# A decoder layer on eight cores: other order and other issue times for the input projections, gate chunks from attention step 8 instead of 14

## The reference, cut to what matters

```python
h = rms_norm(x, norm_mix)                       # x: [2048, 1024] per core
q, k, v, u, g_a, g_p = split(h @ w_in)          # q, k, v, u: 512 columns each; gates: 1024 each
q = rope(rms_norm_per_head(q)); k = rope(rms_norm_per_head(k))
o_attn = moba_attention(q, k, v)                # own block of 256 plus up to 3 selected past blocks
o_pool = multiscale_pool(u)                     # windows 2, 4, 8, 16 minus the token, per-group linear
m = sigmoid(g_a) * (o_attn @ w_up_attn) + sigmoid(g_p) * (o_pool @ w_up_pool)
x = x + m @ w_out
x = x + relu(rms_norm(x) @ w_ff1)**2 @ w_ff2
```

## Time and profile before

| | |
|---|---|
| time, median of 3 runs | 940.35 us (939.48 to 942.74) |
| the profiled execution's own time | 939.31 us |
| span shown by its profile (slowest core) | 938.0 us |
| spans of the 8 cores | 932.2 to 938.0 us |
| granted TensorE clock, mean per core | 0.993 to 1.000 |
| PE busy | 901.4 us (96%) |
| DVE busy | 457.4 us (49%) |
| ACT busy | 368.8 us (39%) |

### The profile page before, as it was taken

One profiled execution on the slowest core, in us unless ns is written; L12 is line 12 of the kernel. 1 busy time (PEld: TensorE's weight loads), 2 busy tenths in 40 slices (PEclk: granted clock), 3 DMA queues, 4 the chain that ended last, 5 costly groups with the idle time before them and its releaser, 6 DMA issues.

```text
span 938.0 us, 17381 instructions; the slowest of 8 cores (932.2 to 938.0 us)
## 1 busy us (share of the span) xinstructions
PE 901.4 (96%) x5724; PEld 461.7 (49%) x5724; DVE 457.4 (49%) x858; ACT 368.8 (39%) x730; POOL 113.2 (12%) x201
## 2 busy tenths in 40 slices
PE   2899998899999999999999999999999999999998
PEld 1444454567777764444444444444444444444444
DVE  2788875656423234334774444444444443444444
ACT  2677545798999962221006234031111221111220
POOL 4212211221000000100101111001110111000000
PEclk9999999999999999999999999999999999999999
DMA  8963342234443444993997434014330333201113
GB/s 199 216 147 88 62 130 52 53 42 83 81 72 58 70 79 107 192 201 80 171 135 117 51 51 55 14 24 56 47 55 1 44 47 57 35 1 68 68 68 157
DMA packets 66341, 78.12 MB, mean 83 GB/s; under 512 B 35984, under 2 KB 54672, under 8 KB 66000
## 3 DMA queue, kind: packets, MB, share of 16 engines
q0 software_dynamic: 25056, 40.28, 29.3%
q1 hardware_dynamic: 41200, 36.75, 16.3%
HBM read 98.41 MB, written 8.39 MB: 114 GB/s over the span
## 4 chain that ended last, share of the span: by engine, by line
PE 89%; DMA 4%; DVE 2%; issue 2%; ACT 2%; DVEq 0%; POOL 0%; ACTq 0%; POOLq 0%; SPq 0%
PE bank L1372 24%; PE bank L1343 24%; PE bank L1013 11%; PE bank L433 9%; PE bank L907 6%; PE bank L1243 6%; PE bank L945 3%; PE bank L1027 3%; PE bank L1032 3%; DMA raw<-x 2%; DMA raw<-w_slice 1%; DMA raw<-w_qkvu 1%; PE bank L487 1%; PE bank L520 1%; DVE raw L461 0%
## 5 line engine op out<-in xcount | busy, mean ns | idle before, releaser
L1350 ACT ACTIVATE raw<-bank 128x512 f32<-128x512 f32 x128 | 76.4, 597 | 375.6 <-PE bank L1343 316.9
L1372 PE MATMUL bank<-raw 128*128 128x512 bf16 (+1 forms) x1032 | 223.2, 377 | 0.0
L1343 PE MATMUL bank<-raw 128*128 128x512 bf16 x1024 | 223.1, 379 | 0.0
L1372 PEld LDWEIGHTS bank<-raw 128*128 128x128 bf16 x1032 | 101.0, 98 | 120.2
L1343 PEld LDWEIGHTS bank<-raw 128*128 128x128 bf16 x1024 | 100.2, 98 | 120.8
L1352 DVE SCALAR_TENSOR_TENSOR raw<-bank,raw 128x512 bf16<-128x512 f32 x128 | 88.6, 692 | 140.6 <-ACT raw L1350 140.6
L914 ACT ACTIVATE raw<-bank 128x512 bf16<-128x512 f32 (+1 forms) x288 | 146.1, 591 | 21.7 <-PE bank L945 20.6
L1380 DVE SCALAR_TENSOR_TENSOR raw<-bank,raw 128x512 f32<-128x512 f32 x129 | 96.3, 747 | 112.5 <-PE bank L1372 112.0
L433 PE MATMUL bank<-raw 128*128 128x512 bf16 x512 | 122.8, 390 | 9.6 <-ACT raw L372 4.0
L1013 PE MATMUL bank<-raw 128*128 128x512 bf16 x512 | 122.5, 379 | 0.7 <-DMA raw<-w_slice 0.7
L907 PE MATMUL bank<-raw 128*128 128x256 bf16 x576 | 98.4, 266 | 2.4 <-ACT raw L914 1.9
(11 more groups left out here) (91 smaller groups left out, 578.5 us busy)
## 6 DMA issues: line engine op xcount, KB each, us to landing
raw<-x SPq DMA_DIRECT2D x32, 512.0 KB, 6.9
raw<-w_ff POOLq DMA_DIRECT2D x64, 256.0 KB, 4.0
raw<-w_slice POOLq DMA_DIRECT2D x22, 640.0 KB, 7.8
out<-raw SPq DMA_DIRECT2D x15, 512.0 KB, 2.6
raw<-w_qkvu POOLq DMA_DIRECT2D x8, 512.0 KB, 12.9
raw<-raw SPq DMA_DIRECT2D x2, 1024.0 KB, 4.8
raw<-w_out POOLq DMA_DIRECT2D x4, 512.0 KB, 13.7
raw<-c_ind POOLq DMA_DIRECT2D x4, 256.0 KB, 4.3
```

The source lines that it names most:

```text
L1343: t.group("pe", [lambda e, c=c, j=j, bk=bk: e.matmul(bank_f(bk), lhsT=ffw1[s][:, c, j * 128:(j + 1) * 128], rhs=hT[:, c, tg * 512:(tg + 1) ...
L1350: t.op("act", lambda e, bk=bk, si_=si_: e.activation(out=sqz[si_], in_=bank_f(bk), func=AF.Square), reads=hb[bk], writes=[b_sqz[si_]])
L1372: t.group("pe", [lambda e, j=j, bk=bk, i=i, c0_=c0_, c1_=c1_, n_=n_: e.matmul(bank_f(bk)[:, 0:n_], lhsT=a1T[ab][:, j, i * 128:(i + 1) * 12 ...
```

## The change

In the first loads, x tile 1 is issued on SP at once, ahead of the wait for K's weights, and V's weights on POOL directly behind the memsets, without a wait for x. The lag of V falls from 3 rounds to 2, that of Q rises from 7 to 8. The U jobs, until now 12 rounds behind K with the last five after all Q jobs, stand in rounds 5, 6, 7, 8, 10 and so on up to 23, every one ahead of the last Q job. U's weights are asked for ahead of Q's, and the band's constants earlier. The planner's assumed arrival times and first free times are other numbers. Gate chunks start at step 8 instead of 14; 92 chunks are still spread up to the same last step, so their distance grows from 3.02 to 3.08 steps.

```diff
-        U_LAG = 12
+        Q_LAG = 8
+        u_round = [int(5.0 + 1.25 * tt) for tt in range(NT)]
         jobs = []
-        for r in range(NT + 7):
-            for cg, lag in ((CG_K, 0), (CG_V, 3), (CG_U, U_LAG), (CG_Q, 7)):
+        for r in range(NT + Q_LAG):
+            for cg, lag in ((CG_K, 0), (CG_V, 2)):
                 if 0 <= r - lag < NT:
                     jobs.append((cg, r - lag))
-        u_rest = list(range(NT + 7 - U_LAG, NT))
+            jobs += [(CG_U, tt) for tt in range(NT) if u_round[tt] == r]
+            if 0 <= r - Q_LAG < NT:
+                jobs.append((CG_Q, r - Q_LAG))
         NJ_Q = len(jobs)
...
             load_w(CG_K)
+            p0_load(1)
             pool_setup()
+            load_w(CG_V)
             t.wait_written("sp", b_wqkvu[CG_K][0])
-            p0_load(1)
             p0_load(2)
...
             p0_load(3)
-            t.wait_written("pool", b_xslot[1])
-            load_w(CG_V)
...
-        W_AT = {CG_K: 15.0, CG_V: 30.0, CG_Q: 43.0, CG_U: 54.0}
-        X_AT = [4.7, 16.3, 18.6, 23.0]
+        W_AT = {CG_K: 14.8, CG_V: 26.0, CG_U: 38.0, CG_Q: 48.0}
+        X_AT = [4.9, 11.5, 17.5, 21.5]
...
-        add("wq", 4.0, [("pool", 2.0, lambda: load_w_after(CG_Q, 0))], deps=[muls[1]], after=26.0)
-        add("wu", 8.0, [("pool", 2.0, lambda: load_w_after(CG_U, 1))], deps=[muls[2]], after=34.0)
+        add("wu", 4.0, [("pool", 2.0, lambda: load_w_after(CG_U, 0))], deps=[muls[1]], after=25.0)
+        add("wq", 8.0, [("pool", 2.0, lambda: load_w_after(CG_Q, 2))], deps=[muls[3]], after=34.0)
...
-        G_START = 14
+        G_START = 8
```

More of the change, by code:

```diff
@@ L417, in p0_ev @@
                   hb[bk], [b_hT[tt]])
-        U_LAG = 12
+        Q_LAG = 8
+        u_round = [int(5.0 + 1.25 * tt) for tt in range(NT)]
         jobs = []
-        for r in range(NT + 7):
-            for cg, lag in ((CG_K, 0), (CG_V, 3), (CG_U, U_LAG), (CG_Q, 7)):
+        for r in range(NT + Q_LAG):
+            for cg, lag in ((CG_K, 0), (CG_V, 2)):
                 if 0 <= r - lag < NT:
                     jobs.append((cg, r - lag))
-        u_rest = list(range(NT + 7 - U_LAG, NT))
+            jobs += [(CG_U, tt) for tt in range(NT) if u_round[tt] == r]
+            if 0 <= r - Q_LAG < NT:
+                jobs.append((CG_Q, r - Q_LAG))
         NJ_Q = len(jobs)
-        for tt in u_rest:
-            jobs.append((CG_U, tt))
+        jobs += [(CG_U, tt) for tt in range(NT) if u_round[tt] >= NT + Q_LAG]
         NJ = len(jobs)
@@ L748, in build_nc @@
         by_job = dict(zip(jobs, pj_of))
-        add("wq", 4.0, [("pool", 2.0, lambda: load_w_after(CG_Q, 0))], deps=[muls[1]], after=26.0)
-        add("wu", 8.0, [("pool", 2.0, lambda: load_w_after(CG_U, 1))], deps=[muls[2]], after=34.0)
-        add("band_ld", 12.0, [("pool", 1.0, lambda: t.dma("pool", band, c_band_d, writes=[b_band]))], after=40.0)
+        add("wu", 4.0, [("pool", 2.0, lambda: load_w_after(CG_U, 0))], deps=[muls[1]], after=25.0)
+        add("wq", 8.0, [("pool", 2.0, lambda: load_w_after(CG_Q, 2))], deps=[muls[3]], after=34.0)
+        add("band_ld", 6.0, [("pool", 1.0, lambda: t.dma("pool", band, c_band_d, writes=[b_band]))], after=27.0)
         add("wg_ld", 20.0, [("pool", 1.0, lambda: t.dma("pool", wgT_f, w_grpT_d, writes=[b_wgTf]))], after=60.0)
@@ L769, in build_nc @@
         free_at = {n_: {i: 0.0 for i in v_} for n_, v_ in pools.items()}
-        eng_free = {"pe": 0.0, "act": 0.0, "dve": 0.0, "pool": 20.0, "sp": 22.0}
+        eng_free = {"pe": 0.0, "act": 0.0, "dve": 0.0, "pool": 17.0, "sp": 21.0}
         INF = 1e18
@@ L1131, in build_nc @@
                 done.add("u")
-                assert si <= 17, si
+                assert si <= 7, si
                 u_done()
```

## The result

The changed kernel is slower: 955.8 us where the prediction has 936.5. Its runs took 950.51, 955.77 and 958.47 us, against a median of 940.61 before; the ratio is 1.0159 (95%: 1.0130 to 1.0188). Two more of its runs, with one die at a lower clock, are left out of every comparison. The profiled execution took 955.77; its slowest core is core 0, its cores spread from 945.8 to 954.7 (before 932.2 to 938.0).

The account below looks back on a forecast made before the run. PE work was taken to bound the kernel, so only its idle time could be won. Four terms, -4.6 + 7.8 - 5.5 - 1.5, gave -3.8: 935.5 us for this execution, 936.5 by the median; 8-in-10 range 930 to 943.

Parts of the forecast that it names:

- What bounds the kernel: Whole kernel: PE work is 89% of the chain, so reordering can win only time in which PE stands still.
- Term 1: Start, up to the 14th finished job: x tile 9 lands at 46, the job ends at 53, -4.6 us (-6.6 to +1.4).
- The third case: Start: V's weights make x tiles land later, tile 9 at 53, sum +5.9, about 946 us; chance 0.20.
- there is room: Start, against the later-tiles case: bytes up to tile 9 are unchanged and the DMA share of the first 60 us is 0.91.
- The cover for K of tile 0: Start: K of tile 0, now held back by tile 1, costs nothing unless tile 1 lands after 13.
- The rule beside it: DMA at the start: engines take turns between queues packet by packet, so V's early issue takes turns from x tiles 2 and 3.
- Term 2: Middle, 14th job to end of last Q job: five more U jobs there, 99.5 against 91.7 us, +7.8 (6.8 to 10.5).
- Term 3: Attention's beginning, last Q job to 18th exponential: ACT's four waits for PE go, -5.5 us (-6.6 to -1).
- My sign of being wrong: Attention's beginning: a granted clock under 0.9 for more than 10 us behind the last Q job would show the forecast wrong.
- The second case: Attention's beginning: without filler PE runs at half speed to the 18th step, sum +0.7, about 941 us; chance 0.26.
- Term 4: Gate chunks: 1.7 more chunks done by step 46 are missing later, where PE is full, -1.5 us (0 to -1.7).

Follow-up runs that it names:

- h2: g1 with V's weights issued without a wait, the order on every engine held fixed: 944.5 us, ratio 1.0057.
- g1: Kernel before with x tile 1 ahead of the wait for K's weights, V's weights behind the landing of x tile 2: 941.7 us, ratio 1.0015.
- h3: f2 with V's weights waiting for x tile 2 again, the planner's order held fixed: 946.3 us, ratio 1.0076.
- f2: Kernel before with only the changed first loads (x tile 1 and V without waits) and their arrival numbers: 948.0 us, ratio 1.0083.
- f4: Changed kernel with the first loads and arrival numbers of before and chunks from step 14, so the order of jobs and weights alone: 946.3 us, ratio 1.0062.
- k5: Kernel before with its own first loads but g1's arrival numbers, so g1's order on every engine: 945.3 us, ratio 1.0061.
- h4: f4 with 25 more products that nobody reads, placed where PE stood still at attention's beginning: 946.1 us, ratio 1.0073.
- h1: f4 with the U jobs spread from round 9 instead of 5, four of them behind the last Q job: 939.9 us, ratio 1.0008.
- k1: Changed kernel with two buffers for the attention outputs instead of one, no load or product moved: 949.8 us, ratio 1.0094.
- g4: f4 with gate slice 1 loaded at step 13 instead of 5: 951.6 us, ratio 1.0115.
- k4: Kernel before with two buffers for the attention outputs instead of one: 939.8 us, ratio 0.9995.

## Why the prediction was wrong

**What bounds the kernel.** That held, as far as PE sets the time: in the ledger the lost PE time goes from 33.2 to 49.6 us up to 260, and the mean span of the cores from 935.5 to 950.0.

**Term 1, the start: -4.6 predicted, +6.6 measured** (64.2 against 57.6). This is the first step that failed. x tile 1 landed at 12.3 (11.5 predicted), and SP's next issue came 1.4 later, as said (1.5). What failed is "up to there x tiles 2 and 3 get the other share ... tiles 7, 8 and 9 take 4.6 each". I took the equal bytes of the earlier trace rows, where both queues had long been busy, for the rate at any time. Where a weight load has just started, x tiles issued 1 to 2.3 us behind it get 0.00 to 0.02 MB in 3 us (15 to 18, 36 to 39; h2 against g1 in one order). Up to tile 6 little is lost by it, 34.5 against my 32. Tile 7 then lands at 46.7, 12.1 behind tile 6 where I had 4.6, and tiles 8 and 9 follow 3.8 and 4.9 behind: 7.5 of the 9.4 us arise at tile 7. The constants behind tile 2 are late too: the rope table lands at 28.8, before at 21.3. The trace of the kernel before had shown it; DMA queues of its core 3, 24 to 25.5, just behind the start of V's weights, with an x tile under way since 23.84:

```profile
q0 software_dynamic: 63, 0.24, 96.4%
q1 hardware_dynamic: 3, 0.00, 0.9%
```

Of the 11.2 us between -4.6 and +6.6, tile 9's landing makes 9.4; the other 1.8 are the step from tile 9 to the 14th job, 8.8 instead of 7. The third case named this mechanism and its point of decision, a landing at 52.5; it came at 55.4, and its formula for the whole sum, landing minus 49.8, would have given +5.6, about 945 for this execution. I gave it 0.20, because "there is room" by the mean DMA share; a mean over 60 us says nothing about the 3 us in which a queue stands.

Nor is the transfer the whole. The order that the planner makes of the new numbers cost 2.4 us with V free, as in the change, and 5.7 with V waiting (h2, h3, g1, f2), and the new order of jobs 3.8 in the first 60 us with before's loads (f4: 24.5 against 20.7); the prediction had no term for either. "The cover for K of tile 0 ... costs nothing unless tile 1 lands after 13" was right, and k5 shows the other side: tile 1 at 16.5 there, and a 9.35 us wait.

**The rule beside it.** The Trainium skill, "DMA: Bandwidth & Descriptors", section "Queues, rings and completion order", has each engine take turns between the queues that have work. The stretches above speak against turns of equal size just behind the start of a weight load: 0.50 against 0.02 MB. Whether the x tiles' queue had work on those engines at that time, no trace here shows. I said that the rule spoke against the change, and its direction was right.

**Term 2: +7.8 predicted, +8.5 measured** (164.3 less 64.2 is 100.1, against 91.7). A little high, inside its range of 6.8 to 10.5, and right.

**Term 3: -5.5 predicted, -6.3 measured** (18.8 against 25.05). The size was right, in part by luck: I had all four waits of ACT gone, and two of 1.59 and 0.81 us are there; but the first exponential comes 4.5 us behind the last Q job where before it came 6.5. My sign of being wrong, a granted clock under 0.9 for more than 10 us, came without the loss: 0.74 from 164 to 184. f4 bears terms 2 and 3 out: over the cores with all matmuls on record they come to +1.9 there (+7.2 and -5.3), against the +2.3 predicted, and its loss is at the start. The second case blamed the clock; h4 shows that the clock is at most a small part. What h1 wins back at this place is the cost that terms 2 and 3 had named together: U jobs moved ahead of the last Q job are paid there in full, and no longer cover DVE's scaling behind it.

**Term 4: -1.5 predicted, +8.0 measured on the slowest core, +4.4 in the mean of the eight** (767.5 against 763.1). This is the second step that failed, by its sign. I counted the chunks' products and their evictions on ACT, and neither what the last chunk of a unit issues, the load of a gate slice on POOL's queue, nor the one `o_tok` behind which DVE and PE can come to stand. The load of the fifth slice hangs on the 25th chunk behind the first and moves by 4.5 steps (from 14 + 3.02 x 25 to 8 + 3.08 x 25); there it lands on the transposes of a finished block, which take 10.4 us for 2.5. That place costs 2.3 us in the mean and 5.8 on core 0, where the granted clock falls behind the wait; so the 8.0 is the worst of eight cores, not the typical one. The wait at the first block costs more in the mean, and no load makes it longer. k1 takes both away, and the kernel is back at 762.9 behind the 18th exponential; g4 makes such a wait worse by moving one load. The kernel before has a slow pair of transposes and a wait as well, and k4 shows that it costs nothing there. Why the same waits are hidden with the chunks of before and not with the earlier ones was not taken apart.

**The sum.** Through the 18th exponential +8.7 instead of -2.3, then +8.0 instead of -1.5: 16.7 against -3.8. In the means of the cores the two wrong terms are +8.2 and +4.4, the two right ones +8.3 and -5.9. The chances followed from a start that I took for a gain.

## What to carry to other kernels

When a step is moved, follow each transfer that it issues, on its own queue, to what else is in flight at that moment: here one load of 640 KB on another queue turned a transfer of 2.5 us into one of 10. Then ask whether anybody waits for it, and behind which buffer: the kernel before has a transfer as slow and loses nothing (k4), while the changed one loses 4.6 us behind one unshared buffer, half of it with no slow transfer at all (k1). A rate read where two queues have long been busy isn't the rate just behind the start of a new load. And where a planner orders the work from arrival numbers, hold the order fixed and change the transfer, then the reverse (g1, h2, h3, k5): otherwise the reshuffle, here as large as the effect sought, is taken for it.

## What the runs showed of the hardware

Two things were not expected. An x tile on the hardware queue, issued 1 to 2.3 us behind a weight load on the software queue, moved 0.00 to 0.02 MB in 3 us where that load had just started, against 0.44 MB without it (g1); afterwards both moved about equal bytes. Why it stands at first is open. And two DMA transposes, 2.4 to 2.6 us alone, take 6.6 to 11.1 us in the kernel before and the changed one when a 640 KB load on the other queue is issued within 0.1 us of the first of them; on the changed kernel's core 0 they land about 0.7 and 1.2 us behind that load. Issued 1.4 us behind the first of two, the load leaves that one at 2.4 to 2.6 and takes the second to 6.5 to 7.8.
